# In the attention of both layers, TensorE's value products of the chunk two behind are put ahead of the turning of the current chunk

## The reference, cut to what matters

```python
sc = (jnp.einsum('bqhd,bshd->bhqs', qn, k_nope)
      + jnp.einsum('bqhe,bse->bhqs', qr, kr)).astype(jnp.float32) * MLA_SCALE
sc = jnp.where(kchunk[None, :] <= qchunk[:, None], sc, NEG)
pr = jax.nn.softmax(sc, axis=-1).astype(v.dtype)
return jnp.einsum('bhqs,bshd->bqhd', pr, v)
```

## Time and profile before

| what | value |
|---|---|
| median of 3 runs | 3198.25 us (3195.41 to 3200.84) |
| the profiled execution: its own time | 3194.3 us |
| the profiled execution: its span | 3192.5 us |
| PE busy over the span | 3006.4 us (94%) |
| DVE busy | 2026.4 us (63%) |
| ACT busy | 982.6 us (31%) |
| POOL busy | 1428.1 us (45%) |
| idle time of DVE's low parts (L2240) before them, <-ACT L1687 | 41.2 us |
| idle time of ACT's high parts (L1687) before them, <-PE L1208 | 48.1 us |

### The profile page before, as it was taken

How to read it: one execution, slowest core, us unless ns; L and a number is a source line. 1 busy time by engine, 2 the same in 40 slices (tenths; PEclk the granted TensorE clock), 3 DMA queues, 4 the chain that set the end, 5 groups by cost and what they waited for, 6 DMA issues and landing times.

```text
span 3192.5 us, 54358 instructions
## 1 busy us (share of the span) xinstructions
PE 3006.4 (94%) x18978; PEld 2905.2 (91%) x18978; DVE 2026.4 (63%) x3685; ACT 982.6 (31%) x2197; POOL 1428.1 (45%) x933
## 2 busy tenths in 40 slices
PE   8999999999999999998989999889899999999887
PEld 7889888888999999998878888889899999999887
DVE  4566888465655565567565588855655655565675
ACT  4234777342000000004442277753300000000252
POOL 4233545464333343345554455545533333343563
PEclk9999999999999999999999999999899999999998
DMA  3497444211111111111103666522011111111111
GB/s 111 178 316 242 123 122 126 98 40 47 40 53 39 46 53 39 46 46 61 40 21 127 187 138 140 130 81 73 28 53 44 42 53 39 46 52 40 48 54 55
DMA packets 163132, 264.63 MB, mean 83 GB/s; under 512 B 95057, under 2 KB 108897, under 8 KB 162641
## 3 DMA queue, kind: packets, MB, share of 16 engines
q1 hardware_dynamic: 163024, 263.21, 26.8%
HBM read 197.74 MB, written 65.42 MB: 82 GB/s over the span
## 4 chain that ended last, share of the span: by engine, by line
PE 78%; DVE 9%; issue 4%; ACT 4%; POOL 3%; DMA 1%; SPq 0%; DVEq 0%; ACTq 0%; POOLq 0%
PE ps L1324 30%; PE ps L1034 12%; PE ps L1035 12%; PE ps L1036 12%; PE ps L1232 4%; PE ps L1208 3%; POOL pre_sums L891 1%; DVE sublayer_out L2058 1%; PE ps L1180 1%; DVE neg_max L2227 1%; DVE out_partial L2252 1%; PE ps L1055 1%; PE ps L1181 1%; PE ps L1069 1%; ACT probs_t_hi L1687 1%
## 5 line engine op out<-in xcount | busy, mean ns | idle before, releaser
L855 POOL TENSOR_TENSOR weight_hi<-weight_raw,ones 128x1024 fp32r<-128x1024 f32 x179 | 354.9, 1982 | 1169.0 <-PE ps L1036 598.8
L2295 DVE TENSOR_TENSOR sublayer_out<-ps,sublayer_out 128x352 f32<-128x352 f32 x1008 | 527.8, 524 | 516.4 <-PE ps L1036 507.9
L1324 PE MATMUL ps<-act_hi,weight_hi 128*128 128x352 f32 x2112 | 686.1, 325 | 10.1 <-ACT ffn_act L1735 4.8
L1324 PE MATMUL ps<-act_hi,weight_lo 128*128 128x352 f32 x2112 | 683.8, 324 | 0.0
L1324 PE MATMUL ps<-act_lo,weight_hi 128*128 128x352 f32 x2112 | 683.7, 324 | 0.0
L869 POOL TENSOR_TENSOR weight_lo<-weight_raw,weight_hi 128x1024 fp32r<-128x1024 f32 x193 | 477.1, 2472 | 54.9 <-ACT weight_hi L1725 28.1
L1034 PE MATMUL ps<-act_hi,weight_hi 128*128 128x352 f32 (+2 forms) x1392 | 469.7, 337 | 29.6 <-DVE weight_lo L2102 11.4
L1035 PE MATMUL ps<-act_lo,weight_hi 128*128 128x352 f32 (+2 forms) x1392 | 457.1, 328 | 0.0
L1036 PE MATMUL ps<-act_hi,weight_lo 128*128 128x352 f32 (+2 forms) x1392 | 456.8, 328 | 0.0
L931 POOL TENSOR_TENSOR probs<-probs,row_inv 128x1024 f32<-128x1024 f32 (+8 forms) x288 | 311.0, 1092 | 322.8 <-DVE row_inv L2235 321.6
L1324 PEld LDWEIGHTS ps<-act_hi,weight_hi 128*128 128x128 f32 x2112 | 399.2, 189 | 14.4 <-issue 6.9
(11 more groups left out here) (177 smaller groups left out, 5763.1 us busy)
## 6 DMA issues: line engine op xcount, KB each, us to landing
weight_raw<-units SPq DMA_DIRECT2D x201, 512.0 KB, 3.3
k_hi<-kB_hi SPq DMA_DIRECT2D x32, 328.0 KB
qA_hi<-stage_hi SPq DMA_DIRECT2D x16, 528.0 KB, 3.4
qA_lo<-stage_lo SPq DMA_DIRECT2D x16, 528.0 KB, 4.5
q_hi<-qA_hi SPq DMA_DIRECT2D x16, 528.0 KB
q_lo<-qA_lo SPq DMA_DIRECT2D x16, 528.0 KB
kA_hi<-stage_hi SPq DMA_DIRECT2D x8, 656.0 KB, 3.0
kA_lo<-stage_lo SPq DMA_DIRECT2D x8, 656.0 KB, 4.7
```

The costliest lines, as they stand in the source:

```text
L855: pool.tensor_tensor(wh[:, slot, :], wraw[:, slot, :], ones[:, 0:1].to_broadcast((P, UW)), ALU.mult).then_inc(w_hi[slot], 1)
L1324: mm = nc.tensor.matmul(ps[:, 3 * slot + b, 0:TB], a, x, start=(k == 0 and pas == 0), stop=(k == KD - 1 and pas == 2))
L2295: V.tensor_tensor(y[:, m, c], src, y[:, m, c], ALU.add).then_inc(f_acc, 1)
```

## The change

The else-branch of the sample's case takes the value products in, and they are dropped behind the turning. For the sample's chunks (4 and 15) the order was so already, and stays.

```diff
                                 turn_waits(i, c, first)
                                 pv(i, c - PV_LAG, first)
+                            elif c >= PV_LAG or not first:
+                                pv(i, c - PV_LAG, first)
                             turn(i, c, first)
-                            if (c >= PV_LAG or not first) and not sample:
-                                pv(i, c - PV_LAG, first)
```

## The result

| | before | changed |
|---|---|---|
| median | 3196.83 us (4 runs, 3190.70 to 3200.84) | 3241.62 us (4 runs, 3239.87 to 3244.17) |
| profiled execution, its span | 3192.5 us | 3242.3 us |

The change makes the kernel slower: ratio 1.0145, 95% interval [1.013, 1.016], which is 45 us. The forecast was 3258, with a range from 3220 to 3290: way and range hold, while the cost was forecast at 62 us above the profiled execution, 17 too much.

What follows compares the result with a forecast made beforehand. Queue order among three heavily loaded engines (PE, DVE, ACT) was taken to bound the attentions. Layer 0's 32.3, layer 1's 28.6 and two drains' 0.5 each made 62 us, added to 3194.3: 3256, adjusted to 3258; range 3220 to 3290.

Steps and rivals of the forecast that it cites:

- The cost is latency, not work: Both attentions: turning starts about 0.48 to 0.85 us later per chunk, so high parts wait for it; gain taken as nothing.
- The first chain: Layer 0, first head: chunk 17's turning late, then exponentials and maximum, until PE idles 0.7 us for a low part.
- The neighbours on PE: Changes of instruction kind on PE: 0.05 to 0.1 us a chunk, about 0.2 us a head reaching the path.
- From S4 to S6: First head: chunk 20's high part 1.2 us late, passed on without slack; scores again wait for about 1 us.
- T1, H1, outputs, L2, V2: Head's end: turning behind last value products, high part 1.76 us late, wait 0.5 for 0.27; first head grows 1.74 us.
- The second head: Layer 0: second head reaches the first's end state, 21.14 us, so it grows by 2.52.
- the heads did not become equal: Sign: heads of equal length, near 21.1 us in layer 0, 20.4 in layer 1; staying unequal would refute the prediction.
- The sum: Both attentions: layer 0 costs 32.3 us, layer 1 28.6, the two drains 0.5 each; 62 us.
- Only the wrap's cost: Rival, both attentions: added latency swallowed except where second heads become like first ones; 20 us, 3217 us; chance 0.12.
- The clock falls: Rival, layer 1 heads and beyond: added waits lower PE's granted clock; up to 24 us, 3282 us; chance 0.15.
- Nothing: Rival, both attentions: the lag of two chunks covers the later turning; 3198 us; chance 0.04.
- Faster: Rival: earlier value products bring outputs and next maximum forward, up to 0.36 us each; 11 us, 3187 us; chance 0.02.

Runs made afterwards that it cites:

- moving it alone: Kernel before, with the new order only for chunks 6 and 17, whose turning then stands behind the sample's value products: 3217.09 us, ratio 1.0061.
- Chunks 1 and 12 alone: Kernel before, with the new order only for chunks 1 and 12, whose turning then follows a head's last value products: 3209.97 us, ratio 1.0045.
- The run without wrap: Kernel before, with slots handed out so that no chunk takes the slot of the chunk two back: 3186.05 us, ratio 0.9969.
- the exchange of partitions: Changed kernel, with outputs of even and odd heads exchanged between lower and upper partitions: one profiled execution, first head 20.24 us, second 20.70 us.
- chunks 9 and 20: Kernel before, with the new order only for chunks 9 and 20: 3204.00 us, ratio 1.0031.

## Why the prediction held, point by point

- **The cost is latency, not work.** Right. Waits for the turning grew from 48.1 to 127.7 us, and the 17.0 us that the high parts waited for value products over both layers went to nothing. On the changed page the mean durations of high and low parts are as before.
- **The first chain.** Right, and well sized up to its end. Counted from the start of the pair, T17 moved by 0.84 us (0.90 forecast), E1 by 0.79 (0.75), N2 by 0.88 (0.94). V18 waits 0.59 us (0.7). That this chunk carries it was shown by moving it alone. S4 then moved by 0.86, not 1.13. The 0.27 were lost in two terms: V18 started 0.1 earlier than followed (8.38 for 8.49 from the pair's start), and the stretch from V18 to S4 took 0.89 us (485.06 to 485.95), not 1.05.
- **The neighbours on PE.** The 0.05 to 0.1 a chunk were the upper end. From the last product of one step's scores to the second of the next, which takes in value products, turning and both changes of kind, a chunk takes 0 to 0.08 us more than before: 1.22 for 1.20 with T16, 1.50 for 1.42 with T17, 0.99 for 0.99 with T18. V18 to T20 takes 0.51 us, for 0.48 from V18 to S4 before. The first 512-column score product behind transpositions holds PE for 0.31 (485.95 to 486.26), for 0.29 behind value products (473.07 to S4's next product at 473.36). The Trainium skill, page "TensorE: Matmul & The Clock Gate", "Architectural detail: the array is 16× 32×32, not 1× 128×128", says that weight loads are pulled ahead of products in flight. If that made the change of neighbours free, as the prediction read it, the trace agrees within 0.02 us for this product, and not for a short one: a 128-column score product holds PE for 0.14 us behind transpositions (482.87 to 483.01) and for 0.06 behind value products (470.83 to 470.89).
- **From S4 to S6.** Right: S6 moved by 0.88, S4 by 0.86, and S6 waits 1.00 us.
- **T1, H1, outputs, L2, V2.** Right in mechanism: V2 moved by 0.47 more (0.52 forecast) and waits 0.53. Chunks 1 and 12 alone cost 0.48 a head.
- **The second head.** This is the step that was mis-sized: "the end state is the same, so it grows by 21.14 - 18.62 = 2.52". It grew by 1.57. The step read the whole difference of 0.78 between the heads as the wrap's. The run without wrap put the wrap at 0.45 and left 0.34. So the heads did not become equal (20.76 and 20.18), which the prediction itself had named as a sign that it was wrong: about 0.58 of the 0.95 is this, and the rest is the first head's 0.4, carried over. In the changed kernel the exchange of partitions shows that the longer head goes with the output operations that write the upper partitions. That the 0.34 of the kernel before has the same cause was not run, and why it is 0.34 there and 0.58 after the change is open.
- **The sum.** Layer 0: 22.9 for 32.3. Layer 1: 22.4 for 28.6. There the first heads last 20.4 us in the mean, as forecast, but by luck: at the full clock they last 19.90, which is the 0.4 of layer 0 again, and the clock in five of the seven fills it up. The 19.38 from which the prediction took their growth was itself a head with a clock of 0.91. The second heads last 19.22 at the full clock, for 20.4.
- **The rivals.** "Only the wrap's cost" is refuted as a sum (20 us for 45), though a wait of its kind is one of the three parts (chunks 9 and 20, 10 us). "The clock falls" did not decide: layer 0 kept 1.00, layer 1 went from 0.95 to 0.94, with eight of fourteen heads at 0.91 or 0.92 for six before, about 1 us of the 45. "Nothing" asked that L18 end before it was needed; V18's wait shows that it doesn't. "Faster" would have needed H20 earlier; it came 0.87 later.

What stays open is why the clock falls in some heads of layer 1 and not in others. In the kernel before, PE waits 1.82 us at S6 of the head from 2005.73, and the granted clock is 0.50 of full (1.2 GHz) from 2020 to 2023; in the head from 2079.85 it waits 1.81 us at the same place, and the head keeps 1.00. In the kernel without wrap that wait is 1.34, and no head fell. No run held the clock fixed.

## What to carry to other kernels

Where an engine gives two pieces of work in a row, one of which others wait for (here the turning, which ACT, DVE and then the engine itself need) and one that nobody waits for soon (the value products), put the first one first, even though both wait for the same semaphore: here the other order cost 45 us. Follow each queue to the next full engine: of the ten chunks of a head whose turning moved by about half a microsecond or more, three made the whole cost. Behind these the trace shows the delay passed on from queue to queue until PE waits for it. And when two stretches with the same instructions differ in length, don't give all of the difference to the first cause found: take that cause away and see what is left. Compare heads at the same granted clock: a 20.4 that agreed with its forecast was 19.90 and a slower clock.

## What the runs showed of the hardware

Behind an output operation on the upper 64 partitions the next ACT or DVE instruction started only when it had ended, and behind one on the lower 64 it mostly overlapped its end. On ACT in the kernel before, E1 starts 0.21 us after the start of a copy of 0.19 us in one case, and in the other the exponentials start 0.16 after it; with the rows exchanged it is 0.22 for the upper partitions and 0.08 for the lower. On DVE in the kernel before, the maximum over 288 keys starts 0.04 us after the end of the output operation ahead of it in the first head and 0.07 before it in the second. The head that has the upper ones is longer by 0.34 to 0.68 us in the kernels whose slots make no difference (0.34 in layer 0 without wrap, 0.58 in layer 0 and 0.68 in layer 1 at the full clock in the changed kernel). Exchanging the source partitions alone (which half of PSUM is read) moved nothing, exchanging the written ones moved the long head. Why, no run shows.
